# One-hot products for the last two expert groups, row gathers beside the experts, and four barriers fewer

## The chip, the cores and the metric

The kernel runs on one core of one Trainium2 chip. The metric is the device time of one launch in microseconds (us). All data are float32. TensorE is called PE in the profile, VectorE DVE, ScalarE ACT, GpSimd POOL, and the queue that loads weights SP.

## The reference, cut to what matters

512 tokens with 1024 features pass through one block of four small mixers with a dense feed-forward part, and then through two blocks of attention with a routed mixture of 16 experts. The change touches only the second half of each of the two routed layers (`l` is 0 or 1):

```python
x = layer_norm(ALPHA * x + mix, ln_g[l, 0], ln_b[l, 0])
ffn = routed_moe(x, router_w, router_b, moe_w_gate[l], moe_w_up[l], moe_w_down[l])
x = layer_norm(ALPHA * x + ffn, ln_g[l, 1], ln_b[l, 1])
```

`routed_moe` picks two experts for each token and weighs their outputs with two gates that sum to one: `y = y + gates[:, e:e+1] * (h @ w_down[e])` with `h = silu(xt @ w_gate[e]) * (xt @ w_up[e])`. The input of layer 1 is the layer norm that ends layer 0, with its gain `ln_g[0, 1]` and bias `ln_b[0, 1]`.

## The kernel before

Every engine runs the same list of stages (`STAGES`, L182): norm1, mixers, mix_out, up, down, gate, then for each of the two routed layers an attention half (even_in to even_out, odd_in to odd_out), route, experts, overflow and combine. Behind most stages the four compute engines meet: each drains, counts up one semaphore and waits for the others (`meet`, e.g. L536). `NO_MEET` (L190) lists the stages without such a barrier. SP stands outside the barriers and loads weights when a semaphore says that a buffer is free.

**Experts.** Each expert owns 96 rows (`CAP`), three tiles of 32. The 1536 rows are cut into 12 groups of 128 (`NG`), so one group holds rows of two experts. For each group POOL gathers the tokens' rows of x from DRAM (L2263), PE transposes them, multiplies with gate and up weights (`enter`, L955), transposes the hidden values (`turn_h`, L973) and multiplies with the down weights (`leave`, L963). The order on PE is enter(g), leave(g-1), turn_h(g), and at last leave(11). ACT copies the 128x1024 result of a group out of PSUM into one of two buffers `y_sb` and stores it to the DRAM tensor `expert_rows` (L1393 to L1402). The 96 MB of weights of a layer come through seven buffers of 2 MB, six of `ring` and `xT`, in an order worked out in advance (`PASSES`, `loads_of`); `FIRST_FREE` (L298) says in which order the buffers are first taken. `load_experts` (L2357) issues the loads on SP as the passes free buffers. Rows beyond 96 of an expert go to `overflow`, a loop over `over_n` slots that each engine reads into a register (`slots_of`, L318).

**Route.** DVE works out in some 80 small operations each token's two experts, ranks and places (`route`, L1935, and `place_tokens`, L2000, which runs at the start of the experts). Among them is `at_rank`, a 128x128 one-hot matrix per token tile and choice that PE multiplies with token numbers to get the list of tokens of each group (L924).

**Combine.** Behind the barriers of experts and overflow, POOL loads the layer norm's gain and bias rows (L2187), and then issues eight gathers of 128 rows from `expert_rows` (L2295; two choices, four token tiles). For each tile ACT weighs the first row (L1189), DVE adds the second with its weight (`mul_add`, L1517, called at L2063), adds `ALPHA * x` (L2064), and runs `norm_tile` (L1541): two batch statistics, aggregate, epsilon; ACT takes the root (L1147); DVE centres (L1557), inverts the root and applies gain and bias (L1569). In layer 0 PE transposes the finished tile (`turn_tile`, L556), and ACT copies it into xT (L1152), from which the next stage, `odd_in`, starts. In layer 1 SP writes each tile to the output.

**The attention stages' weights.** `chunks` are numbered weight pieces and chunk `at` lies in ring slot `at % RING`. The seven pieces of the odd attention (29 to 35) are loaded by `load` (L2327) once their slot's last holder among the experts is done. `odd_out` (`halves`, L755, on PE; `residual`, L1581, on DVE) multiplies with two halves of `w_o` and adds the residual.

Of the kernel before, what the change touches and what calls it, by code (L numbers as in the profile page):

```python
# [27 lines left out]
P = 128  # L28
T = 512
# [17 lines left out]
NG = E * CAP // P  # L47
OVER_K = -(-(T - CAP) // P)
# [37 lines left out]
def packs(i):  # L86
# [17 lines left out]
        ("token_f", (np.arange(NT)[None, :] * P + q[:, None]).astype(f)),  # L104
        ("norm1", cols(i["norm1_g"])),
# [84 lines left out]
NO_MEET = ("even_out", "route0", "odd_out", "route1")  # L190
# [6 lines left out]
def build(nc, w, pk_shapes, out, stop=None):  # L197
# [3 lines left out]
    with ctx:  # L201
# [28 lines left out]
        weight = sb("weight", [P, 2, NT])  # L230
# [58 lines left out]

        def experts_of(g):  # L290

            return [(4 * g + i) // 3 for i in range(4)]
# [5 lines left out]
        FIRST_FREE = [(5, 2, 0, 1, 3, 4, RING), (2, 3, 0, 1, 4, 5, RING)]  # L298
# [13 lines left out]

        def expert_buffer(b, k):
# [9 lines left out]
        def slot_view(at, c):  # L323
            nk, ncols = c[2], c[4]
            return ring[:, at % RING, 0:nk * ncols].rearrange("p (k n) -> p k n", k=nk)
# [33 lines left out]
        y_rows = Area().take(2, NT, D)  # L359
# [64 lines left out]
        scaled_p, probsT_done, sinks_in = sem("scaled_p"), sem("probsT_done"), sem("sinks_in")  # L424
        probsT_taken = sem("probsT_taken")
        pair_done, out_done, out_taken, bias_row = sem("pair_done"), sem("out_done"), sem("out_taken"), sem("bias_row")
# [8 lines left out]
        rows_gathered = [sem(f"rows_gathered{n}") for n in range(NT)]  # L435
        idx_cleared, idx_loaded, x_stored = sem("idx_cleared"), sem("idx_loaded"), sem("x_stored")
# [7 lines left out]
        first_weighed = sem("first_weighed")  # L444
# [49 lines left out]
        def summed(j):  # L494

            m = HC - j
            if j < 8:
# [25 lines left out]
        idx_one = sb("idx_one", [P, 1], U32)  # L523
        over_w = ea.take(2, SLOT)
        y_cleared = sem("y_cleared")

        over = {n: sem(f"over_{n}") for n in ("idx", "in", "xT_mm", "xT", "gate_up_mm", "silu", "h", "hT_mm", "hT", "down_in",
                                              "y_mm", "y", "stored", "passed", "all_stored")}
# [4 lines left out]
        def _(pe):  # L533
# [8 lines left out]
            def arrived(at):  # L542
                pe.wait_ge(w_loaded[at % RING], 16 * (at // RING + 1))
# [434 lines left out]

            def experts(l):

                turn_x(l, 0)
                for g in range(NG):
                    enter(l, g)
                    if g:
                        leave(l, g - 1)
                    turn_h(l, g)
                leave(l, NG - 1)

            def overflow(l):

                n, done = slots_of(pe, l)
                gate_w, up_w = (over_w[:, i, :].rearrange("p (k n) -> p k n", k=KD) for i in range(2))
                down_w = over_w[:, 0, :].rearrange("p (k n) -> p k n", k=4)
                with pe.If(n > 0):
                    with pe.Fori(0, n) as slot:
# [17 lines left out]
                        for i in range(2):  # L1013
                            product(banks[5 + i][:, :], [(hidT[:, t, :], down_w[:, t, i * 512:(i + 1) * 512])
                                                         for t in range(4)]).then_inc(over["y_mm"], 1)

            def combine(l):
                if l == 0:
# [99 lines left out]
        def _(act):  # L1118
# [37 lines left out]
            def norm_tiles(stage, before=None):  # L1156
                for n in range(NT + 2):
# [4 lines left out]
                    if n >= 2 and stage not in FEATURE_GAIN and stage != "combine1":  # L1162
# [23 lines left out]
            def combine(l):  # L1186
                def weigh_first(n):
                    act.wait_ge(rows_gathered[n], 32 * (l + 1))
                    A(y_rows[:, 0, n, :], y_rows[:, 0, n, :], ACT.Copy, scale=weight[:, 0, n:n + 1]).then_inc(first_weighed, 1)  # L1189

                norm_tiles(f"combine{l}", weigh_first)
# [187 lines left out]
            def experts(l):  # L1379
                take_x(NG * l)  # L1380
                for g in range(NG):
# [5 lines left out]
                    if g:  # L1387
                        leave(l, g - 1)
                leave(l, NG - 1)
                for b in range(2):  # L1390
                    act.wait_ge(y_stored[b], 16 * (NG // 2) * (l + 1))

            def leave(l, g):  # L1393

                at = NG * l + g
                if at >= 2:
                    act.wait_ge(y_stored[g % 2], 16 * (at // 2))
# [3 lines left out]
                act.wait_ge(y_taken, 2 * at + 2)  # L1401
                act.dma_start(y_dram[g * P:(g + 1) * P, :], y_sb[:, g % 2, :]).then_inc(y_stored[g % 2], 16)  # L1402

            def overflow(l):
                n, done = slots_of(act, l)
                with act.If(n > 0):
                    with act.Fori(0, n) as slot:
# [7 lines left out]
                        for g in range(2):  # L1415
                            act.wait_ge(over["y_mm"], j * 2 + g + 1)
                            step_in(A(y_sb[:, 0, g * 512:(g + 1) * 512], banks[5 + g][:, :], ACT.Copy), j * 2 + g + 1)
                        act.dma_start(y_dram[bass.ds(slot * P + NG * P, P), :], y_sb[:, 0, :]).then_inc(over["stored"], 16)

                    act.wait_ge(over["stored"], (n + done) * 16 + 16)  # L1420
                    act.sem_inc(over["all_stored"], 1)
# [77 lines left out]
        def _(dve):  # L1499
# [81 lines left out]
            def residual(name, scale, loads=0):  # L1581

                f = F[name]
                for k in range(10):
                    if k < 8:
# [349 lines left out]
            def route(l):  # L1935
# [62 lines left out]
                V.tensor_copy(idx_sb[:, 0:NG], banks[5][:, 0:NG]).then_inc(idx_ready, 1)  # L1998

            def place_tokens(l):  # L2000
# [25 lines left out]
                step(V.reciprocal(wsum, wsum))  # L2026
                for j in range(2):
                    step(V.tensor_tensor(weight[:, j, :], weight[:, j, :], wsum, ALU.mult))
# [8 lines left out]
                step(V.tensor_copy(over_list[:, :], e_list))  # L2037

            def experts(l):
                place_tokens(l)  # L2040
                for at in range(NG * l, NG * (l + 1)):
# [4 lines left out]
                    V.tensor_copy(hidT.rearrange("p a b -> p (a b)"), banks[4][:, :]).then_inc(hT_ready, 1)  # L2046

            def overflow(l):
                n, done = slots_of(dve, l)
                with dve.If(n > 0):  # L2050
                    with dve.Fori(0, n) as slot:
# [5 lines left out]
                        V.tensor_copy(hidT.rearrange("p a b -> p (a b)"), banks[4][:, :]).then_inc(over["hT"], 1)  # L2057

            def combine(l):
                for n in range(NT):  # L2060
# [373 lines left out]
```

## Time and profile before

| | us |
|---|---|
| median of 3 runs | 2189.02 (2188.75 to 2190.48) |
| the profiled execution | 2186.29 |
| its span, first to last instruction | 2184.6 |
| PE / DVE / ACT / POOL busy | 1953.7 / 658.8 / 398.3 / 81.1 |

The times are device times of whole launches. The span is that of one execution that was recorded instruction by instruction; its own time is 1.7 us above its span. PE is busy for 89% of the span; the granted TensorE clock was 0.928 of full speed on average. The DMA queues moved 336.59 MB.

### The profile page before, as it was taken

What the parts mean: (1) busy time and instruction counts of PE and PEld (TensorE: products, weight loads), DVE (VectorE), ACT (ScalarE), POOL (GpSimd) and SP (SyncE); (2) the same over time, 40 slices, a digit from 0 to 9 for tenths busy, and PEclk for the clock granted to TensorE, in tenths of its full rate; (3) what the DMA queues carried; (4) which work ended last, traced back from release to release, by engine and by line L of the source; (5) the groups of instructions that cost most, each with busy time, mean ns of one, the idle gap of its engine ahead of it and who ended that gap; (6) DMA issues with size and microseconds to landing.
All of it is one profiled execution on the core that took longest, in us unless ns stands there. A gap on an engine that the chain in (4) does not pass through costs nothing.

```text
span 2184.6 us, 23031 instructions
## 1 busy us (share of the span) xinstructions
PE 1953.7 (89%) x9622; PEld 877.2 (40%) x9622; DVE 658.8 (30%) x1564; ACT 398.3 (18%) x853; POOL 81.1 (4%) x104
## 2 busy tenths in 40 slices
PE   7999999999999998979997999955988997999991
PEld 3454444444444444435552333312644444333230
DVE  3736312233200331116343000005676625000005
ACT  3213011111100022016410111101125511111111
POOL 0000010000000000000002000010000000200001
PEclk9989999999999999987897999986999996999996
DMA  4104532221212213110234999963100233899973
GB/s 147 64 20 145 183 135 77 77 77 68 77 58 77 71 39 116 39 39 1 97 131 155 392 398 399 394 246 128 39 0 1 78 145 135 279 398 398 395 293 154
DMA packets 140920, 336.59 MB, mean 154 GB/s; under 512 B 4568, under 2 KB 12776, under 8 KB 140688
## 3 DMA queue, kind: packets, MB, share of 16 engines
q1 hardware_dynamic: 126384, 283.80, 35.3%
q0 software_dynamic: 10688, 36.71, 4.4%
q10 hardware_dynamic: 3744, 14.59, 1.6%
q8 instruction: 78, 1.28, 0.2%
q14 instruction: 26, 0.21, 0.0%
HBM read 310.93 MB, written 24.14 MB: 153 GB/s over the span
## 4 chain that ended last, share of the span: by engine, by line
PE 76%; issue 8%; DMA 7%; DVE 6%; ACT 2%; POOL 0%; DVEq 0%; another core or an unknown queue 0%; POOLq 0%; PEldq 0%; ACTq 0%; SPq 0%
PE psum L553 31%; PE psum L951 20%; PE psum L796 7%; DMA ring<-in_moe_w_up 5%; PE psum L733 5%; PE psum L862 3%; PE psum L890 2%; PE psum L875 2%; PE psum L932 1%; DVE small L1546 1%; PE psum L565 1%; DMA scratch<-expert_rows,place 1%; PE psum L675 1%; ACT ring L1357 1%; DVE x L1517 1%
## 5 line engine op out<-in xcount | busy, mean ns | idle before, releaser
L951 PE MATMUL psum<-ring,scratch 128*32 128x512 f32 x3840 | 518.1, 602 | 13.3 <-DMA ring<-in_moe_w_up 8.9
L553 PE MATMUL psum<-xT,ring 128*128 128x512 f32 (+2 forms) x1056 | 465.5, 601 | 8.2 <-PE psum L553 3.4
L553 PEld LDWEIGHTS psum<-xT,ring 128*128 128x128 f32 (+2 forms) x1056 | 199.5, 190 | 271.7 <-issue 270.8
L951 PEld LDWEIGHTS psum<-ring,scratch 128*32 128x32 f32 x3840 | 144.3, 111 | 301.5 <-issue 296.4
L553 PE MATMUL psum<-ring,xT 128*128 128x512 f32 (+4 forms) x704 | 239.8, 497 | 2.5 <-ACTq L1124 1.6
L553 PEld LDWEIGHTS psum<-ring,xT 128*128 128x128 f32 x704 | 120.3, 194 | 120.0 <-issue 111.8
L796 PE MATMUL psum<-ring,scratch 128*128 128x512 f32 x352 | 155.7, 603 | 4.0 <-remote 3.3
L951 PE MATMUL psum<-xT,scratch 128*32 128x512 f32 x768 | 129.3, 603 | 8.4 <-DMA ring<-in_moe_w_up 8.4
L1517 DVE SCALAR_TENSOR_TENSOR scratch<-psum,overlay,scratch 128x511 f32<-128x511 f32 x88 | 65.9, 749 | 232.0 <-ACT scratch L1288 230.4
L2044 DVE TENSOR_TENSOR scratch<-psum,scratch 128x512 f32<-128x512 f32 x24 | 16.6, 692 | 345.9 <-PE psum L951 345.9
L733 PE MATMUL psum<-xT,ring 128*128 128x512 f32 x224 | 104.4, 623 | 2.4 <-DVEq L1506 2.3
L796 PEld LDWEIGHTS psum<-ring,scratch 128*128 128x128 f32 x352 | 67.4, 193 | 91.6 <-issue 91.6
L1517 DVE SCALAR_TENSOR_TENSOR x<-x,psum 128x512 f32<-128x512 f32 x32 | 22.0, 688 | 269.0 <-PE psum L796 141.2
L862 PE MATMUL psum<-scratch 64*128 64x256 f32 (+11 forms) x256 | 76.4, 522 | 14.9 <-POOLq L2171 10.2
L1288 ACT ACTIVATE scratch<-psum,overlay 128x512 f32<-128x512 f32 x44 | 34.2, 777 | 270.2 <-PE psum L553 270.2
L553 PE MATMUL psum<-ring,scratch 128*128 128x512 f32 x160 | 72.6, 606 | 2.9 <-DVEq L1506 1.6
L1147 ACT ACTIVATE small<-small 128x1 f32<-128x1 f32 x28 | 5.7, 203 | 377.2 <-DVE small L1553 377.2
L1345 ACT ACTIVATE ring<-ring,small 128x257 f32<-128x257 f32 (+5 forms) x128 | 68.0, 538 | 8.1 <-DVE small L1905 8.0
L2046 DVE COPY scratch<-psum 128x512 f32<-128x512 f32 x24 | 16.6, 692 | 172.9 <-PE psum L976 172.9
L565 PE MATMUL psum<-base,x 128*128 128x128 f32 x128 | 22.3, 334 | 51.4 <-DVE x L1569 46.9
L733 PEld LDWEIGHTS psum<-xT,ring 128*128 128x128 f32 x224 | 44.5, 201 | 57.2 <-issue 56.9
L1377 ACT ACTIVATE scratch<-psum 128x512 f32<-128x512 f32 x48 | 26.3, 595 | 210.9 <-PE psum L932 210.9
(339 smaller groups left out, 1612.8 us busy)
## 6 DMA issues: line engine op xcount, KB each, us to landing
ring<-in_moe_w_gate SPq DMA_DIRECT2D x28, 2048.0 KB, 15.1
ring<-in_moe_w_up SPq DMA_DIRECT2D x28, 2048.0 KB, 17.4
ring<-in_moe_w_down SPq DMA_DIRECT2D x24, 2048.0 KB, 15.6
ring<-in_w_up SPq DMA_DIRECT2D x11, 2048.0 KB, 7.7
xT<-in_moe_w_down SPq DMA_DIRECT2D x8, 2048.0 KB, 11.5
expert_rows<-scratch ACTq DMA_DIRECT2D x24, 512.0 KB, 7.4
ring<-in_w_down SPq DMA_DIRECT2D x4, 2048.0 KB, 7.8
ring<-in_even_w_in SPq DMA_DIRECT2D x4, 2048.0 KB, 7.6
```

The costliest lines, as they stand in the source:

```text
L553: mm = nc.tensor.matmul(out_, lhsT, rhs, start=(j == 0), stop=(j == len(pairs) - 1))
L565: mm = nc.tensor.transpose(banks[turn_bank(stage, n) + j][:, t * P:(t + 1) * P], src[:, (4 * j + t) * P:(4 * j + t + 1) * P], ident)
L733: mm = nc.tensor.matmul(banks[k % 2][:, :], lhsT, rhs, start=(t == 0), stop=(t == KD - 1))
L796: mm = nc.tensor.matmul(banks[4 * half_ + n][:, :], hidden[:, k0 + t, n * P:(n + 1) * P], w_[:, t, :], start=(k0 + t == 0), stop=(k0 + t = ...
L862: mm = nc.tensor.matmul(banks[2 * (p % 2) + hh][:, 0:span(kind, n)[1]], head_q(kind, n, j, hh), head_k(kind, n, j, hh), start=True, stop=True)
L875: mm = nc.tensor.transpose(banks[4 + u % 2][:, b * P:(b + 1) * P], probs[:, u % 6, b * P:(b + 1) * P], ident)
L890: mm = nc.tensor.matmul(banks[6 + g % 2][r, c], head_v(kind, s0 // P + b, h), probsT[:, (2 * p + hh) % 4, b * P:(b + 1) * P], start=(b == ...
L951: mm = nc.tensor.matmul(bank[r, :], lhsT[:, t, r], w_[:, t, c0:c0 + 512], start=(t == 0), stop=(t == nk - 1))
L1288: A(conv[:, k % 4, :], banks[k % 8][:, :], ACT.Identity, bias=operand["fconv_b"][:, k:k + 1], scale=w3[:, k, 2:3]).then_inc(f.a, 1)
L1345: A(to, of, ACT.Exp, bias=negmax[:, u % 8:u % 8 + 1], accum_out=p_total[:, u % 8:u % 8 + 1])\
L1377: A(xgT[:, 4 * h:4 * h + 4, :].rearrange("p a b -> p (a b)"), banks[h][:, :], ACT.Copy).then_inc(xgT_ready, 1)
L1517: return V.scalar_tensor_tensor(out_, in0, s, in1, ALU.mult, ALU.add)
```

## The change

- `NE = NG - 2 = 10`. Groups 0 to 9 are stored to DRAM as before. Groups 10 and 11 are not stored; they stay in the two buffers `y_sb`, and their slots in `expert_rows` are zeroed at the start, together with those of the overflow (12 clearing DMAs of 512 KB in the stage `up`, before 10).
- The eight row gathers are issued at the end of POOL's `experts`, once the stores of groups 0 to 9 have landed, into a memory area of their own (the overflow's weight buffers). DVE adds them to x behind its last work on the experts, eight `mul_add` of 128x1024, with weights that are zero for places outside the ten groups.
- `share_late` on PE, between enter(0) and turn_h(0): eight one-hot products of 2 columns that give each row of groups 10 and 11 its gate weight. `seek_late` on DVE, behind its first group: two matrices `late_hot` of 128x512, row by token, that hold the weight where row and token belong together.
- `combine`: PE multiplies `late_hot` with `y_sb` into PSUM, for each of four token tiles two groups and two halves (16 products of 128x512). DVE adds PSUM to x and sums the row in one operation; ACT squares the centred row and sums it, and takes the root. In layer 0 DVE only centres and scales x; gain and bias are applied feature by feature where the transposed tile is copied into xT, half of it by ACT, half by DVE. The gain and bias that x itself still lacks are applied in `odd_out`, on the first four steps of `residual` (`gain`). In layer 1 gain and bias rows are loaded into a ring slot after the last gate pass.
- The weights are divided by ALPHA in `place_tokens`, so that `ALPHA * x` is no step of its own; the epsilon is divided by ALPHA squared.
- experts0, overflow0, experts1 and overflow1 join `NO_MEET`; each engine reads the overflow count near the end of `experts`.
- The odd attention's pieces lie in slots 2, 3, 1, 4, 5, 2, 3, and `FIRST_FREE` of layer 1 is 4, 5, 0, 1, 2, 3 with xT last.

```diff
+NE = NG - 2
-NO_MEET = ("even_out", "route0", "odd_out", "route1")
+NO_MEET = ("even_out", "route0", "experts0", "overflow0", "odd_out", "route1", "experts1", "overflow1")
...
+        ODD_SLOTS = (2, 3, 1, 4, 5, 2, 3)
-        FIRST_FREE = [(5, 2, 0, 1, 3, 4, RING), (2, 3, 0, 1, 4, 5, RING)]
+        FIRST_FREE = [(5, 2, 0, 1, 3, 4, RING), (4, 5, 0, 1, 2, 3, RING)]
...
+            def share_late(l):
+                pe.wait_ge(late_w, l + 1)
+                for j in range(2):
+                    for n in range(NT):
+                        mm = nc.tensor.matmul(banks[7][:, 0:2], at_rank[:, j, n, :], late_share[:, NT * j + n, :],
+                                              start=(j == 0 and n == 0), stop=(j == 1 and n == NT - 1))
+                mm.then_inc(late_mm, 1)
...
                     enter(l, g)
-                    if g:
+                    if g == 0:
+                        share_late(l)
+                    else:
                         leave(l, g - 1)
                     turn_h(l, g)
+                pe.wait_ge(over_known, l + 1)
+                slots[l] = slots_of(pe, l)
                 leave(l, NG - 1)
...
             def combine(l):
+                for n in range(NT):
+                    for g in range(2):
+                        for h in range(2):
+                            if n == 0 and h == 0:
+                                pe.wait_ge(late_ready, 2 * l + g + 1)
+                            if n == 0:
+                                pe.wait_ge(y_taken, 2 * (NG * l + NE + g) + h + 1)
+                            mm = nc.tensor.matmul(banks[2 * n + h][:, :], late_hot[g][:, n * P:(n + 1) * P],
+                                                  y_sb[:, g, h * 512:(h + 1) * 512], start=(g == 0), stop=(g == 1))
+                    mm.then_inc(late_done, 1)
                 if l == 0:
                     for n in range(NT):
                         turn_tile("combine0", n)
...
+                def spread(n):
+                    act.wait_ge(tile_var, base + n + 1)
+                    step(A(y_rows[:, 0, n, :], x[:, n, :], ACT.Square, bias=mean[:, n:n + 1], accum_out=sumsq[:, n:n + 1]))
+                    A(rstd[:, n:n + 1], sumsq[:, n:n + 1], ACT.Sqrt, scale=1.0 / D, bias=moe_eps).then_inc(tile_sd, 1)
+                def take(n):
+                    act.wait_ge(tile_turned, base + n + 1)
+                    for k in range(KD // 2):
+                        ins = A(xT[:, k, n * P:(n + 1) * P], banks[2 * n][:, k * P:(k + 1) * P], ACT.Identity,
+                                scale=operand["moe_g"][:, k:k + 1], bias=operand["moe_b"][:, k:k + 1])
+                    ins.then_inc(tile_taken, 1)
...
+                slots[l] = slots_of(dve, l)
+                for n in range(NT):
+                    dve.wait_ge(rows_gathered[n], 32 * (l + 1))
+                    step(mul_add(x[:, n, :], y_rows[:, 0, n, :], early_weight[:, 0, n:n + 1], x[:, n, :]))
+                    mul_add(x[:, n, :], y_rows[:, 1, n, :], early_weight[:, 1, n:n + 1], x[:, n, :]).then_inc(early_added, 1)
...
+                def gather_sum(n):
+                    dve.wait_ge(late_done, NT * l + n + 1)
+                    step(V.tensor_tensor_reduce(x[:, n, :], psum[:, 2 * n:2 * n + 2, :].rearrange("p b q -> p (b q)"), x[:, n, :],
+                                                1.0, 0.0, ALU.add, ALU.add, total(n)))
+                    V.tensor_scalar(back(n), total(n), -1.0 / D, None, ALU.mult).then_inc(tile_var, 1)
+                    if l == 1:
...
+                        centred[n] = begun(V.scalar_tensor_tensor(y_rows[:, 1, n, :], x[:, n, :], back(n), end_g, ALU.add, ALU.mult))
+                def scale(n):
+                    r = rstd[:, n:n + 1]
+                    dve.wait_ge(tile_sd, base + n + 1)
+                    step(V.reciprocal(r, r))
+                    if l == 0:
+                        V.tensor_scalar(x[:, n, :], x[:, n, :], back(n), r, ALU.add, ALU.mult).then_inc(tile_ready, 1)
+                    else:
+                        finished(centred[n])
+                        V.scalar_tensor_tensor(x[:, n, :], y_rows[:, 1, n, :], r, end_b, ALU.mult, ALU.add).then_inc(tile_ready, 1)
+                def take(n):
+                    dve.wait_ge(tile_turned, base + n + 1)
+                    for k in range(KD // 2, KD):
+                        V.tensor_scalar(xT[:, k, n * P:(n + 1) * P], banks[2 * n + 1][:, (k - 4) * P:(k - 3) * P],
+                                        operand["moe_g"][:, k:k + 1], operand["moe_b"][:, k:k + 1], ALU.mult, ALU.add)
+                for n in range(NT + 2):
+                    if n < NT:
+                        gather_sum(n)
+                    if 1 <= n <= NT:
+                        scale(n - 1)
+                    if n >= 2 and l == 0:
+                        take(n - 2)
...
+                def gain(n):
+                    dve.wait_ge(moe_rows, 32)
+                    step(V.tensor_tensor(x[:, n, :], x[:, n, :], affine_g, ALU.mult))
+                    step(V.tensor_tensor(x[:, n, :], x[:, n, :], affine_b, ALU.add))
...
+                pool.wait_ge(late_ready, 2 * (l + 1))
+                if l == 1:
+                    pool.wait_ge(gate_up_done, 2 * (NG * l + NG - 1) + 1)
+                    for i, n in enumerate(("ln_g_1_1", "ln_b_1_1")):
+                        pool.dma_start(ring[:, END_ROWS, i * D:(i + 1) * D], w[n]).then_inc(moe_rows, 16)
+                for b in range(2):
+                    pool.wait_ge(y_stored[b], 16 * (NE // 2) * (l + 1))
+                gather_rows(lambda n: rows_gathered[n])
```

## Rows read from the trace of the kernel before

**Rows 1.** The chain that ended last, layer 0: start us, us, what.
```profile
1423.29 20.74 PE psum L951 x192
1445.40 7.12 PE psum L951 x64
1453.17 7.24 DMA expert_rows<-scratch
1465.62 10.55 DMA scratch<-expert_rows,place
1508.67 31.83 PE psum L553 x112
```

**Rows 2.** The same chain, layer 1.
```profile
2108.94 20.74 PE psum L951 x192
2138.81 2.62 DMA expert_rows<-scratch
2147.47 4.96 DMA scratch<-expert_rows,place
2153.72 1.30 DVE scratch L1517
2174.52 1.29 DVE scratch L1517
2180.24 1.29 DVE x L1569
```

**Rows 3.** Stretches of 10 us: engine busy (x instructions), granted clock, DMA share, GB/s.
```profile
1190.00:1200.00 10.00, 9.76 (x80) 2.87 (x76) 0.00 (x0) 0.60 (x1) 5.78 (x6) 1.00 0.37 54
1200.00:1210.00 10.00, 10.00 (x91) 3.42 (x82) 0.69 (x1) 1.83 (x4) 1.06 (x2) 1.00 1.04 364
...
1430.00:1440.00 10.00, 10.00 (x99) 3.00 (x94) 0.69 (x1) 0.60 (x1) 0.00 (x0) 1.00 0.26 106
...
1460.00:1470.00 10.00, 0.00 (x0) 0.00 (x0) 0.00 (x0) 0.00 (x0) 5.60 (x7) 0.50 1.05 406
...
1510.00:1520.00 10.00, 10.00 (x20) 3.21 (x19) 1.37 (x2) 0.00 (x0) 0.00 (x0) 0.84 0.01 2
```

**Rows 4.** POOL in order of time, layer 1, the last of eight gathers.
```profile
2154.95 0.94 POOL L2295 DMA_INDIRECT scratch<-expert_rows,place  x1 [0.30 <-issue]
```

**Rows 5.** DMA issues: median us to landing; gathers of layer 0, then layer 1.
```profile
expert_rows<-scratch ACTq DMA_DIRECT2D x24, 512.0 KB, 7.4
...
scratch<-expert_rows,place POOLq DMA_INDIRECT x8, 12.6
...
scratch<-expert_rows,place POOLq DMA_INDIRECT x8, 5.8
```

**Rows 6.** Groups of instructions by form: x count | busy us, mean ns.
```profile
L1517 DVE SCALAR_TENSOR_TENSOR scratch<-scratch,weight 128x1024 f32<-128x1024 f32 x8 | 10.2, 1280 | 54.8 <-ACT scratch L1189 54.8
L1901 DVE CUSTOM_DVE_ANT_0 ring<-psum,base 128x512 f32<-128x512 f32 x16 | 10.4, 689 | 8.2 <-PE psum L862 8.2
L1564 DVE TENSOR_SCALAR scratch<-x,small 128x1024 f32<-128x1024 f32 x8 | 6.0, 753 | 0.3
L1176 ACT ACTIVATE scratch<-x 128x1024 f32<-128x1024 f32 x4 | 4.2, 1056 | 4.1 <-DMA x<-in_x 3.9
L1357 ACT ACTIVATE ring<-psum 128x128 f32<-128x128 f32 x32 | 7.3, 275 | 11.9 <-PE psum L875 11.8
L1147 ACT ACT_TABLE_LOAD x10 | 12.8, 1283 | 3.0 <-DVEq L1506 2.4 <-ACTq L1124 0.3
```

**Rows 7.** PE in order of time: products at L924, transposes at full clock.
```profile
1133.82 1.07 PE L565 MATMUL psum<-base,x 128*128 128x128 f32 x8
...
1156.50 3.58 PE L924 MATMUL psum<-scratch 128*128 128x12 f32 x16 [2.93 <-DVE scratch L1995]
```

**Rows 8.** The chain: a count read into PE's register, and odd_out's first half.
```profile
1460.64 0.49 PEldq L320
...
1757.55 27.74 PE psum L553 x64
```

More of the change, by code:

```diff
@@ L104, in packs @@
         ("token_f", (np.arange(NT)[None, :] * P + q[:, None]).astype(f)),
+        ("tile_row", rows(np.arange(NT, dtype=f) * P)),
+        ("moe_g", cols(i["ln_g_2"][0, 1])), ("moe_b", cols(i["ln_b_2"][0, 1])),
         ("norm1", cols(i["norm1_g"])),
@@ L311, in build @@
                     holder[b] = LAST_USE[m, e], PASSES[LAST_USE[m, e]]
+        END_ROWS = buffer_of[1]["gate", E - 1][0]
+        assert END_ROWS < RING and LAST_USE["gate", E - 1] == PASSES.index(("gate", NG - 1))
         def expert_buffer(b, k):
@@ L1161, in norm_tiles @@
                         root_tile(stage, n)
-                    if n >= 2 and stage not in FEATURE_GAIN and stage != "combine1":
+                    if n >= 2 and stage not in FEATURE_GAIN:
                         take_tile(stage, n - 2)
@@ L1416, in overflow @@
                             act.wait_ge(over["y_mm"], j * 2 + g + 1)
[L1417 to L1421, printed above, removed]
+                            step_in(A(y_over[:, g * 512:(g + 1) * 512], banks[5 + g][:, :], ACT.Copy), j * 2 + g + 1)
+                        act.dma_start(y_dram[bass.ds(slot * P + NG * P, P), :], y_over).then_inc(over["stored"], 16)
             def step_in(ins, value):
@@ L1579, in take_tile, with residual @@
                 ins.then_inc(tile_taken, 1)
-            def residual(name, scale, loads=0):
+            def residual(name, scale, loads=0, first=None):
                 f = F[name]
                 for k in range(10):
+                    if first and k < NT:
+                        first(k)
                     if k < 8:
@@ L2141, in out_stage @@
             def out_stage(name, loads):
-                residual(name, ALPHA, loads)
+                def gain(n):
+                    dve.wait_ge(moe_rows, 32)
+                    step(V.tensor_tensor(x[:, n, :], x[:, n, :], affine_g, ALU.mult))
+                    step(V.tensor_tensor(x[:, n, :], x[:, n, :], affine_b, ALU.add))
+                residual(name, ALPHA, loads, gain if name == "odd_out" else None)
             run = {
@@ L2289, in overflow @@
                         pool.dma_start(over_w[:, 0, :].rearrange("p (k n) -> p k n", k=4), src[0]).then_inc(over["down_in"], 16)
[L2291 to L2297 removed]
+                    pool.wait_ge(over["stored"], (n + done) * 16 + 16)
+                    pool.sem_inc(over["passed"], 1)
+                    gather_rows(lambda n: over_rows[l])
             run = {
```

155 lines of the change are left out of this document (105 added, 50 removed).

## The prediction

> **What bounds the kernel now.** I read the chain of waits first, at the end of either routed layer, then the table of 10 us stretches, then POOL's and the DMA issues' rows, and last the prices by form. The chain shows one serial tail per layer. In layer 0, PE's last product of the experts starts at 1445.40 and ends at 1452.5; ACT copies; the store takes 7.24; the engines meet; the first gathers take 10.55 more; then DVE works through four tiles; odd_in's first product starts only at 1508.67 [rows 1]. So 56 us pass between the end of the experts and the next stage, in which PE does nothing but transposes: its busy time is 0.00 and its clock 0.50 at 1460 to 1470 [rows 3]. Layer 1 has the same tail, from 2138.2 to 2184.6, with faster transfers (2.62 and 4.96) and one tile each 6.93 us (from 2153.72 to 2174.52 it is three tiles) [rows 2]. Before the tail the experts are bound by the DMA engines: from about 1200 the DMA share is 1.04, and only at 1430 to 1440 does it fall to 0.26 [rows 3]. The change works on both tails, and puts a little into the stretch that feeds the DMA-bound phase.
>
> All that follows is in the clock of the profiled execution.
>
> **Layer 0, what is added ahead of the tail.** `share_late` is eight products with a full 128x128 left side and 2 columns. The nearest row is L924, the same left side with 12 columns, 16 records (eight products) in 3.58, at a low clock [rows 7]; eight transposes at full clock, 1.07, are the low end. PE is at full clock there [rows 3], so I take about half of 3.58, 1.9. It stands on PE before turn_h(0), where DVE has the hidden values ready at about the same time, so nothing covers it. Whether it is paid depends on the DMA engines: at 1190 to 1200 their share is only 0.37 [rows 3], because the loads wait for buffers that PE frees. The loads start 1.9 later and the DMA-bound phase moves along: +1.9, with zero and 3.6 as ends. `place_tokens` grows by four small operations behind work that already ends before the first group's hidden values are needed; they and `seek_late` (two comparisons and two scalings of 128x512, some 2.5 us on DVE once per layer) are hidden in PE's 13.9 us of the next gate and up products. The register reads (0.49 is the longest one in the chain [rows 8]) come while PE waits for DVE's copy of the last hidden values; what sticks out I take as 0.1 in layer 0 and 0.5 in layer 1, where two counts are read, and the branch around the overflow as 0.3 each.
>
> **Layer 0, the tail anew.** PE: down(11) ends at 1452.5 + 1.9 + 0.4 = 1454.8. The 16 late products cost as much each as odd_out's, 27.74 for 64 records or 32 products [rows 8], 0.867: 3.5 per token tile, 13.9 in all. They follow without a gap, so at full clock. Tile 0 is there at 1458.3, tile 3 at 1468.7.
> DVE: free when down(11) starts, 1447.3, plus 0.9 for its register read. Eight additions of 128x1024 at 1.280 [rows 6] with 0.03 between them are 10.5: 1458.7, just with tile 0.
> The gathers: down(9) ends where the 20.74 of 192 records begin, 1423.3 [rows 1]; with 1.9, ACT's copy and a store of 7.4 [rows 5] that is 1433.2. Eight issues at 0.94 + 0.30 [rows 4] last until 1443.1. They move 4.2 MB. The odd pieces come beside them: two (3.55 MB) once gate(11) is done at 1432.1, two more (2.9 MB) seven us later. Together 10.6 MB at 406 GB/s [rows 3] take 26 us; with half the engines the gathers need 4.2 / 0.203 = 20.7 and are in at about 1454. Counted by landings it is 1443.1 + 12.6 [rows 5] = 1455.7. DVE wants the last tile at 1448.2 + 7.9 = 1456.1. It fits, barely; a few us of delay would still be covered by PE's late products, until 1468.7.
> The end: PE transposes only behind all late products, so from 1468.7. Four transposed tiles cost 1.07 each at full clock [rows 7]. From there DVE sets the pace: take(0) begins at 1469.9 and costs 1.1 (four pieces of 128x128; only ACT has a row for such a piece, 0.275 [rows 6]; I take it for DVE too, between 0.8 and 1.5 for the four). gather_sum is twice the 0.689 of the summing operation from PSUM, less one overhead, and a small one: 1.45. scale is 0.753 for a 128x1024 TENSOR_SCALAR and a reciprocal: 0.95 [rows 6]. ACT's square (1.056 and 0.19 for the sum) and one table load of 1.283 [rows 6] lie behind PE's first tiles. So 1469.9 + take 1.1 + sum(3) 1.45 + scale(2) 0.95 + take 1.1 + scale(3) 0.95 + take 1.1 + take 1.1 = 1477.7, 0.5 for a last transpose that is late, 0.7 for the meeting: odd_in starts at 1478.9 instead of 1508.67. **Layer 0 gives 29.8.**
>
> **Between the layers.** `gain` puts eight DVE operations of 128x1024, about 1.23 each or 9.8, on the first four steps of odd_out, where PE needs 27.74 for the first half [rows 8] and DVE has 0.7 of work per tile. Its row loads wait behind nothing but two others on POOL; even landing 15 us late they leave DVE level with PE by the fourth tile. Cost 0; uncovered it would be 9.8. The ring order: piece 34 now waits for 29 and 35 for 30, both used up more than 100 us before odd_out; layer 1's first expert buffers are again those of the two latent pieces. Cost 0. Two more clearing DMAs lie in `up`, 0.
>
> **Layer 1.** share_late again 1.9, reads and branch 0.8. down(11) starts at 2108.94 + 20.74 + 1.37 (the same gap as in layer 0) = 2131.05 and ends at 2138.2 [rows 2]. PE has tile 0 at 2138.2 + 2.7 + 3.5 = 2144.4 and tile 3 at 2154.8. POOL waits for gate(11), 2115.9 + 1.9, loads two rows (1.2), issues gathers from 2119.3 to 2129.2; landing 5.8 [rows 5], 2135. DVE: 2131.0 + 1.9 + 1.3 = 2134.2, additions to 2144.7, branch to 2145.0. Then per tile sum 1.45, centring 1.25, reciprocal 0.1, scaling 1.25: 4.05, of which PE's 3.5 and ACT's 1.5 are covered; four are 16.2: 2161.2. Behind DVE's last operation come 3.1 for the output (2180.24 + 1.29 to 2184.6 [rows 2]): 2164.3. **Layer 1 gives 20.3.**
>
> **Sum.** 29.8 + 20.3 = 50.1; the profiled execution's 2186.3 becomes 2136.2. The median of the runs lies 2.7 above it, so I forecast 2139.
>
> **Two rules of the Trainium skill.** POOL's gather issues keep their 0.94 us and a pitch of 1.24 up to the last one at 2154.95 [rows 4], although DVE's additions had run since 2153.72 [rows 2]. The Trainium skill, SBUF — State Buffer, section "SBUF: two separate sides", speaks against this change: while VectorE runs an operation in a two-port mode, GpSimd can't write the descriptors of its DMAs, which then start late. By that rule gathers beside DVE work would stretch; by the row they don't beside SCALAR_TENSOR_TENSOR, and in the new place DVE has 0.69 us of PSUM work in 7 us. The sum would be the same unless other modes come in.
> The first pair of gathers took 10.55 beside the odd pieces and 4.96 alone [rows 1, 2]. The Trainium skill, DMA: Bandwidth & Descriptors, section "Queues, rings and completion order", says that a DMA engine takes turns between the queues that have work, a packet at a time. By it the gathers get half; packets of unequal size would make it less, which is the first rival.
>
> **Rivals.**
> *Gathers late in layer 0* (15%). For it: 12.6 against 5.8 [rows 5]. Against: PE's late products cover until 1468.7. If the gathers get through only behind the odd pieces' 6.4 MB (16 us), the last lands at 1470; DVE ends its additions at 1472.6 and has four tiles of 3.5 and a transpose before it, 1488.4: 9.5 less gain, 2148.5.
> *Late products at half clock* (7%). The clock was 0.50 in this place before [rows 3], but behind 10 idle us. If the waits at tile 0 let it fall, 32 products cost 27.8 more, all on the path: 2167.
> *The change doesn't do what it says* (4%): the gathers still start only behind the experts. Then only the barriers (about 4 each) and DVE's shorter tiles remain: layer 0 8.7, layer 1 4.6, 2176.
> *Slower* (3%): the clock doesn't come back. Late products at half clock take 27.8 of the 50.1, and if PE stays there into odd_in, each us of its full-clock work costs one more. It decides from 22 us of such work on; a chain stretch like the 31.83 at 1508.67 [rows 1] and the next one would make 2139 + 27.8 + 60 = 2227. Against it: before, the clock was back at 0.84 over 1510 to 1520 [rows 3], after longer idleness.
>
> **How the numbers follow.** The forecast holds 70%; 1% is for small debts that cancel it. The low end is its own with share_late and reads at nothing (-5), odd_in finding the clock up (-2) and takes at 0.8 (-2), and a little more: 2128. The high end takes in late gathers and most of a half-clock tail: 2162; 5% lie above for the serial case and the slower one, 4% partly above for half clock, a few below. A change within 0.2% (4.4 us) can't be told from none by this measurement: 1%. Faster 96%, slower 3%.
>
> **What would show it.** In the trace after: eight gathers on POOL that begin near 1433 and near 2119; a block of late products of 13.9 us right behind down(11) at clock 1.00, with no store between; odd_in's first product some 24 us behind the end of down(11), not 56; each layer 1 tile about 4.05 us apart on DVE instead of 6.93; the DMA-bound phase as long as before and some 2 us later. Wrong: PE idle ahead of the late products, DVE waiting for gathers beyond 1459, an expert phase that grew by more than 3 us, or a PE wait in odd_out for DVE.

## Result and the profile after

The changed kernel runs in 2131.7 us (median of 4, 2130.6 to 2134.1) against 2189.8 (median of 4): a ratio of 0.9741, 95% interval 0.9728 to 0.9754. It is faster by 58 us. The forecast was 50 us faster, 2139, with a range of 2128 to 2162. The profiled execution has a span of 2129.4, 55.2 below that of before.

The chain of waits of the changed kernel, both tails (start us, us, what; the lines that answer to [rows 1] and [rows 2]):

```profile
1155.12 4.20 DMA scratch<-x_rows,idx_sb
...
1417.96 20.74 PE psum L978 x192
1440.07 7.07 PE psum L978 x64
1447.15 13.93 PE psum L1072 x32
1471.63 34.98 PE psum L580 x112
1506.61 10.24 PE psum L1095 x24
...
1724.96 27.74 PE psum L580 x64
...
2076.46 20.74 PE psum L978 x192
2098.56 7.07 PE psum L978 x64
2105.64 7.08 PE psum L1072 x16
```

The store, the gathers and the barriers have left the chain. In layer 0 the late products (L1072) stand right behind down(11), and odd_in starts 24.5 us behind that product's end, where it was 56. In layer 1 the chain leaves PE after two tiles and goes on over DVE. Its timeline (start us, us, engine, line, operation), with POOL's first gathers of either layer:

```profile
1426.40 0.93 POOL L2442 DMA_INDIRECT scratch<-expert_rows,place  x1 [63.56 <-DMA expert_rows<-scratch]
...
2085.53 0.99 POOL L2442 DMA_INDIRECT scratch<-expert_rows,place  x1 [0.30 <-issue]
```

```profile
1440.26 7.64 DVE L1591 SCALAR_TENSOR_TENSOR x<-scratch,early_weight,x 128x1024 f32<-128x1024 f32 x6 [0.24 <-issue]
1448.06 2.61 DVE L1591 SCALAR_TENSOR_TENSOR x<-scratch,early_weight,x 128x1024 f32<-128x1024 f32 x2 [0.16 <-DMA scratch<-expert_rows,place]
1450.82 1.23 DVE L2181 CUSTOM_DVE_ANT_0 x<-psum,x 128x1024 f32<-128x1024 f32 x1 [0.15 <-PE psum L1072]
...
2099.11 10.15 DVE L1591 SCALAR_TENSOR_TENSOR x<-scratch,early_weight,x 128x1024 f32<-128x1024 f32 x8 [0.60 <-issue]
...
2116.79 1.22 DVE L2181 CUSTOM_DVE_ANT_0 x<-psum,x 128x1024 f32<-128x1024 f32 x1
...
2120.83 1.22 DVE L2181 CUSTOM_DVE_ANT_0 x<-psum,x 128x1024 f32<-128x1024 f32 x1
```

All eight row sets are there in time: in layer 0 DVE waits 0.16 us for one of them, in layer 1 for none, and its eight additions end just as PE has the first tile. In layer 1 a tile takes 4.04 us on DVE (2116.79 to 2120.83) instead of 6.93 [rows 2]. PE's clock behind the experts, in stretches of 10 us (busy, granted clock, DMA share, GB/s; compare [rows 3]):

```profile
1440.00:1450.00 10.00, 9.93 (x71) 3.42 (x72) 9.46 (x9) 1.19 (x2) 0.00 (x0) 1.00 1.04 401
1450.00:1460.00 10.00, 10.00 (x24) 4.37 (x23) 6.57 (x14) 5.22 (x8) 0.00 (x0) 1.00 0.58 222
1460.00:1470.00 10.00, 5.89 (x35) 4.43 (x33) 7.13 (x21) 6.64 (x19) 0.00 (x0) 0.85 0.00 0
1470.00:1480.00 10.00, 8.37 (x14) 2.51 (x15) 1.23 (x4) 1.37 (x4) 1.04 (x2) 0.64 0.01 2
```

Where the span's 55.2 us went, stage by stage, from the two chains:

| stretch | before | after | less by |
|---|---|---|---|
| start to the first token gather of layer 0 | 1160.57 | 1155.12 | 5.4 |
| experts 0, to the start of group 11 | 262.72 | 262.84 | -0.1 |
| group 11 to odd_in's first product | 85.38 | 53.67 | 31.7 |
| odd_in to odd_out's first product | 248.88 | 253.33 | -4.4 |
| odd_out and route 1 | 86.19 | 86.28 | -0.1 |
| experts 1, to the start of group 11 | 265.20 | 265.22 | 0.0 |
| group 11 to the end | 75.66 | 52.94 | 22.7 |

The two tails give 54.4. The first row and the fourth are stretches in which the change adds next to no work (two clearing DMAs in the first block); the experiments tell the two apart. Single times of one kernel spread by up to 18 us in the later measurements (2183.5 to 2201.3 for the kernel of before), so the traces' stretches carry the verdicts below and the medians stand beside them. "Tail 0" and "tail 1" are the table's third and last stretch.

### The profile page after: what moved, and what is told of

It reads as the page before. It is cut to its first block, busy times and chain, and to the rows that moved or that the text cites. A ratio compares the mean times of both kernels' runs of the same rounds, so it can differ in the third digit from the quotient of the medians.

```text
span 2129.4 us, 23221 instructions
## 1 busy us (share of the span) xinstructions
PE 1977.8 (93%) x9718; PEld 890.7 (42%) x9718; DVE 671.2 (32%) x1600; ACT 402.5 (19%) x869; POOL 82.1 (4%) x106
## 4 chain that ended last, share of the span: by engine, by line
PE 79%; issue 8%; DMA 6%; DVE 5%; ACT 2%; POOL 0%; DVEq 0%; another core or an unknown queue 0%; ACTq 0%; POOLq 0%; SPq 0%
PE psum L580 32%; PE psum L978 20%; PE psum L823 7%; DMA ring<-in_moe_w_up 5%; PE psum L760 5%; PE psum L889 3%; PE psum L917 2%; PE psum L902 2%; PE psum L1072 1%; PE psum L959 1%; PE psum L702 1%; PE psum L592 1%; ACT ring L1429 1%; PE psum L1003 0%; PE psum L1095 0%
## 5 line engine op out<-in xcount | busy, mean ns | idle before, releaser
L978 PE MATMUL psum<-ring,scratch 128*32 128x512 f32 x3840 | 513.9, 602 | 14.4 <-DMA ring<-in_moe_w_up 11.4
L823 PEld LDWEIGHTS psum<-ring,scratch 128*128 128x128 f32 x352 | 67.4, 193 | 91.6 <-issue 91.6
L889 PE MATMUL psum<-scratch 64*128 64x256 f32 (+11 forms) x256 | 77.1, 529 | 14.2 <-POOLq L2326 10.2
L917 PE MATMUL psum<-ring,scratch 128*64 128x128 f32 x592 | 52.3, 308 | 9.3 <-ACT ring L1429 9.1
```

Of the source, the lines that this page charges most:

```text
L823: mm = nc.tensor.matmul(banks[4 * half_ + n][:, :], hidden[:, k0 + t, n * P:(n + 1) * P], w_[:, t, :], start=(k0 + t == 0), stop=(k0 + t = ...
L889: mm = nc.tensor.matmul(banks[2 * (p % 2) + hh][:, 0:span(kind, n)[1]], head_q(kind, n, j, hh), head_k(kind, n, j, hh), start=True, stop=True)
L917: mm = nc.tensor.matmul(banks[6 + g % 2][r, c], head_v(kind, s0 // P + b, h), probsT[:, (2 * p + hh) % 4, b * P:(b + 1) * P], start=(b == ...
L978: mm = nc.tensor.matmul(bank[r, :], lhsT[:, t, r], w_[:, t, c0:c0 + 512], start=(t == 0), stop=(t == nk - 1))
```

## Experiments

**Both kernels again.** No edit.

> The changed kernel once more, to see what of the difference belongs to the change. The profile of the change shows the first block (up to the even attention's product at 1069.21) 5.4 us earlier than before, at a granted clock that fell less often in the mixers; no edit touches that part. If that is chance of the clock's phase, first-block ends will spread by several us from one execution to the next, of either kernel. If it belongs to the program (another length of the code or another layout), every kernel with this first block ends it near 1069, and the one of before near 1074.6. Time by both: 2131 to 2134 us.

> The kernel of before once more with a profile. If the first block's 5.4 us belong to the program, the even attention's product begins near 1074.6 again and odd_in's first product needs about 31.8 us for its 112 records again; if they are chance of the clock's phase, one or the other differs by some us.

Measured: 2135.3 us for the change (4 runs, 2127.5 to 2137.3) against 2186.5 (7 runs), ratio 0.9754 (0.9721 to 0.9788), a gain of 51.1 where the first measurement had 58.0; and one profiled run of before, 2188.6. The chains, first of the change, then of before:

```profile
1160.07 4.17 DMA scratch<-x_rows,idx_sb
...
1476.90 34.96 PE psum L580 x112
```

```profile
1157.70 4.20 DMA scratch<-x_rows,idx_sb
...
1509.08 31.85 PE psum L553 x112
```

The first gather starts at 1160.1 now where it was 1155.1, in the same kernel, and at 1157.7 in the kernel of before where it was 1160.6. Over the eleven traces of kernels with the changed first block (two of the change and nine of its variants) it lies near one of three values, 1154.5 to 1155.1, 1157.5 to 1157.9 or 1160.1 to 1161.2, and both traces of before fit the same values. So the 5.4 us are chance. PE's busy time up to 1150 goes with it, from 1076.8 to 1081.9 us, so PE's work takes longer in the late ones. The 3.1 us more in odd_in's first 112 records are not chance: 31.83 and 31.85 before, 34.96 to 34.99 in all eight traces with the change and no filler; the filler experiment shows where they lie. The tails repeat within 0.1 (53.66 and 52.91) for the change and within 0.8 for before.

**The barriers back.**

```diff
-NO_MEET = ("even_out", "route0", "experts0", "overflow0", "odd_out", "route1", "experts1", "overflow1")
+NO_MEET = ("even_out", "route0", "odd_out", "route1")
```

> The changed kernel with the four barriers behind experts and overflow put back (two per layer). Theory (the barriers' removal is worth something because it lets PE's late products start beside DVE's additions of the gathered rows): PE can start them only when DVE is through with its additions, 3 to 4 us after down(11), plus two meetings of 0.5 to 1 us: 4 to 6 us per layer, 8 to 12 in all, 2141 to 2144 us. Rival (barriers cost only their own semaphores, some 1 us each): 2 to 4 us, 2134 to 2136.

Measured: 2147.2 us (11.8 above the change measured beside it); tail 0 60.5 (+6.8), tail 1 59.9 (+7.0). The chain, and PE's clock in stretches of 4 us:

```profile
1448.71 1.28 DVE x L1591
...
1450.88 16.63 PE psum L1072 x32
```

```profile
1448.00:1452.00 4.00, 1.12 (x2) 0.63 (x3) 1.96 (x2) 0.00 (x0) 0.00 (x0) 0.68 1.05 390
1452.00:1456.00 4.00, 4.00 (x6) 1.55 (x5) 0.00 (x0) 0.00 (x0) 0.00 (x0) 0.50 0.67 263
```

The theory's direction holds, and its size was too small: 4 to 6 us per layer were expected. PE waits for the end of DVE's additions, 4.2 us in all, and then its late products take 16.63 instead of 13.93, at a clock that had fallen to 0.50 behind that wait; this 2.7 was no term of the theory. From the end of the additions (1449.99) to the first late product are 0.9 us: the barriers' own semaphores are the smallest part.

**The gathers behind the experts.**

```diff
+                pool.wait_ge(y_taken, 2 * NG * (l + 1))
                 gather_rows(lambda n: rows_gathered[n])
```

> The changed kernel, but POOL issues the row gathers only when ACT has taken the last expert group out of PSUM, so nothing of them lies beside the experts. Theory (the overlap of the gathers is the largest part of the gain): layer 0 ends its additions near 1466 instead of 1450.7 and loses about 11 us after what PE's late products cover, layer 1 about 14 us: 2131.7 + 25 = 2157, between 2150 and 2162. Rival (PE's late products of 13.9 us cover them anyway): below 2140.

Measured: 2155.4 us (20.1 above the change measured beside it); tail 0 65.4 (+11.7), tail 1 67.7 (+14.7), 26.4 together. DVE now waits for the transfers:

```profile
1463.14 2.61 DVE L1591 SCALAR_TENSOR_TENSOR x<-scratch,early_weight,x 128x1024 f32<-128x1024 f32 x2 [14.99 <-DMA scratch<-expert_rows,place]
1466.72 7.71 DVE L1591 SCALAR_TENSOR_TENSOR x<-scratch,early_weight,x 128x1024 f32<-128x1024 f32 x6 [0.97 <-DMA scratch<-expert_rows,place]
```

Both tails moved as expected. The traced execution, 2164.5, is the slowest of the four, though; the others lie at 2152.8 to 2157.0. So the overlap of the gathers is worth 26 us by the trace, about half of the 54.4, and 20 by the medians; one trace can't say which is typical.

**Late products twice.**

```diff
                 for n in range(NT):
+                    for _ in range(2):
                     for g in range(2):
```

(with the loop's body indented)

> The changed kernel with every group of late one-hot products done twice (the second overwrites the first, same output). Theory for layer 0: PE's late products are on the path as a whole (transposes stand behind them), so all 13.9 us more show. For layer 1: DVE's 4.05 us per tile is the pace now and PE's 3.5 hides under it; doubled, PE's 6.9 becomes the pace, and the end moves by about 12.5. Sum 26, 2158 us. Rival (DVE's additions and its four tiles are the path in both layers, PE is beside them): less than 14 us in all.

Measured: 2159.8 us (24.5 above the change); tail 0 67.4 (+13.7), tail 1 65.5 (+12.5). Both numbers are those of the theory:

```profile
1452.71 27.66 PE psum L1073 x64
...
2121.83 27.68 PE psum L1073 x64
2149.53 1.22 DVE x L2182
```

In layer 0 every us of late products is paid. In layer 1 the last sum now starts as PE's last product ends (2149.53), and 1.2 of the 13.7 added are hidden; that they lay under DVE's 4.04 per tile is the theory's reading of it.

These three experiments don't cover the whole tail. What the store that left the chain (7.24 and 2.62 us [rows 1, 2]) and the shorter work per tile gave by themselves, and what the new places of the weights in the ring did, no run tells apart.

**The 2-column products more often.** `share_late` repeats its eight products 4 and 12 times.

```diff
+                for _ in range(4):
                 for j in range(2):
```

> The changed kernel with the one-hot products of 2 columns behind the first group done four times (same result), 5.5 us more on PE per layer, ahead of turn_h(0). The forecast took the single ones as paid in full (1.9 per layer), because the loads there wait for buffers that PE frees; the trace shows an expert phase no longer than before. Theory (the weight stream sets the phase's length and PE has some 10 us of waits for it per layer, so delays near its start are absorbed): below 3 us in all. Rival (the delay moves the loads along, and a single 1.84 happened to fall in a gap): about 11 us.

> The same products twelve times, 20 us more on PE per layer. By the theory that the weight stream hides PE's delay up to about 10 us per layer, some 10 us per layer show, 20 in all (12 to 28). By the rival that the delay moves the loads along, all of it shows, 40 us. If even this costs nothing, PE is nowhere near the bound in the experts.

Measured: 2157.9 and 2208.5 us. With x4 the expert phases are 272.9 and 271.2 (+9.3 and +7.6 on the mean of 263.6 over the seven traces with single products at the first group, 262.1 to 265.2; PE's products became 7.7 and 7.5 longer). Another 5 us lie in the odd attention of that execution (258.2), where the granted clock was 0.90 over its last 42 us and 1.00 in the change; this is not explained. With x12 the phases are 300.5 and 299.4, 36 to 37 more, where the products became 34.9 longer. The theory of the first text (below 3 us) is wrong and its rival is right: what PE loses here is paid in full. And PE loses more than the count says, so that the rival's 11 and 40 us were too small as well. In order of time, x12:

```profile
1184.58 36.77 PE L1013 MATMUL psum<-scratch 128*128 128x2 f32 x192
```

and its stretches:

```profile
1190.00:1200.00 10.00, 10.00 (x48) 10.00 (x48) 0.00 (x0) 0.00 (x0) 5.65 (x6) 0.50 0.18 53
1200.00:1210.00 10.00, 10.00 (x49) 10.00 (x48) 0.00 (x0) 0.00 (x0) 0.25 (x1) 0.50 0.20 53
1210.00:1220.00 10.00, 10.00 (x49) 10.00 (x48) 0.00 (x0) 0.00 (x0) 0.00 (x0) 0.50 0.01 2
```

A record costs 0.191 us, against 0.149 in x4 and 0.115 in the single set: PE is busy all the time, with weight loads of 128x128 and two columns behind each, and the granted clock is 0.50. The DMA share falls to 0.01: SP issues no weight load from 1190 to 1225, since its loads wait for buffers that PE frees.

**The 2-column products at the ninth group.**

```diff
-                    if g == 0:
-                        share_late(l)
-                    else:
+                    if g:
                         leave(l, g - 1)
+                    if g == 8:
+                        share_late(l)
...
-                    if at == NG * l:
+                    if at == NG * l + 8:
                         seek_late(l)
```

> The changed kernel with the one-hot products of 2 columns (and what DVE makes of them) moved from the first group to the ninth, where PE has waits for the weight stream behind it. Done 4 and 12 times at the first group they cost as much as PE's own time, and yet the change's expert phases (262.8 and 265.2 us from the first gather to the last group) are no longer than those of before (262.7 and 265.2; 265.7 and 265.4 in another execution). Theory (the single 1.84 us is paid, and hidden in the 3 us by which the phase varies): the phases become about 1.8 shorter each, near 261.5 on average, 3.7 us of the time. Rival (a delay below some us is absorbed because the stream isn't waiting for just these buffers): no difference.

Measured: 2132.2 us (6 runs, 2131.4 to 2138.9), phases 261.5 and 264.3; with the last kernel's 261.8 and 264.4 (below) a mean of 263.0 against 263.6. The theory's 1.8 per phase did not show, but this is inconclusive: 0.6 us lies well inside the spread of 3, and 1.8 can't be excluded.

**Filler products.**

```diff
                 if l == 0:
+                    def fill(count):
+                        pe.wait_ge(tile_taken, norm_base["combine0"] + 1)
+                        for _ in range(count):
+                            nc.tensor.matmul(banks[0][:, :], ident, causal, start=True, stop=True)
                     for n in range(NT):
                         turn_tile("combine0", n)
+                        if n:
+                            fill((0, 2, 1, 2)[n])
```

> The changed kernel with five products of 128x512 on PE that nobody reads, put into the gaps between the transposes in layer 0's combine (two after tile 1, one after tile 2, two after tile 3), so that PE is not idle ahead of odd_in. In the change's trace odd_in's first 112 records need 34.98 us against 27.7 + 3 at full clock, and the clock is 0.50 at 1472 to 1476 and again near 1500. Theory (the clock fell because of the gaps, the low stretch at the start can be bought off): 2 to 4 us faster than the change, clock near 1.00 at odd_in's start. Rival (the low stretches come with the kind of work, or wherever the clock's phase falls): no faster; or slower by up to 1 us where a filler delays a transpose.

> The filler kernel once more beside the other two: its median was level with the change's although its trace showed 6.4 us less behind the filler. Theory: the gain is real and was covered by the first block's chance 6 us; 2126 to 2130 us here, and 246.9 again from odd_in's to odd_out's start. Rival: the filler only sometimes keeps the clock up; then this trace shows about 253.

Measured: 2132.2 us (5 runs, 2123.8 to 2136.2; ratio to before 0.9740, 0.9724 to 0.9757) and 2129.6 (4 runs; 0.9732, 0.9698 to 0.9767). The stretches of the first:

```profile
1464.00:1468.00 4.00, 3.63 (x16) 1.74 (x15) 3.89 (x13) 3.38 (x9) 0.00 (x0) 1.00 0.02 4
1468.00:1472.00 4.00, 3.69 (x15) 1.70 (x14) 2.22 (x7) 2.36 (x7) 0.97 (x2) 1.00 0.00 0
1472.00:1476.00 4.00, 4.00 (x10) 1.23 (x9) 0.00 (x0) 0.00 (x0) 0.07 (x1) 1.00 0.00 0
...
1496.00:1500.00 4.00, 4.00 (x26) 4.00 (x25) 0.00 (x0) 0.17 (x1) 0.00 (x0) 0.65 0.02 4
```

The clock stays at 1.00 until some 24 us into odd_in; its first 112 records take 29.43 and 31.19 instead of 34.97, and the stretch from odd_in to odd_out is 246.9 and 248.2, against 253.0 to 253.3. So the filler gives 5 to 6 us in the traces, where 2 to 4 were expected. In the medians it lies between 0.5 above and 5.8 below the change, which these runs don't separate.

The 112 records are 48 of 512 columns and then 64 of four columns. Split there (us from first start to first start, and to the end), the loss of the change and the gain of the filler lie in different places:

| | the 48 | the 64 |
|---|---|---|
| before, two traces | 23.10, 23.31 | 8.73, 8.54 |
| change without filler, eight traces | 23.37 to 23.68 | 11.31 to 11.59 |
| with filler, two traces | 20.82, 20.82 | 8.61, 10.37 |

The 64, in order of time, before and after, and the clock over a part of them:

```profile
1531.77 8.73 PE L553 MATMUL psum<-ring,xT 128*128 128x4 f32 x64
1495.20 11.40 PE L580 MATMUL psum<-ring,xT 128*128 128x4 f32 x64
```

```profile
1531.80:1536.00 4.20, 4.20 (x40) 4.20 (x38) 0.89 (x2) 0.35 (x2) 0.00 (x0) 1.00 0.00 0
1536.00:1540.40 4.40, 4.40 (x28) 4.40 (x27) 0.00 (x0) 0.17 (x1) 0.00 (x0) 0.63 0.00 0
```

```profile
1495.00:1499.00 4.00, 4.00 (x30) 3.79 (x29) 0.89 (x2) 0.17 (x1) 0.00 (x0) 0.83 0.00 0
1499.00:1503.00 4.00, 4.00 (x20) 4.00 (x21) 0.00 (x0) 0.17 (x1) 0.00 (x0) 0.50 0.00 0
```

The low clock at odd_in's start, worth 2.3 to 2.9 us, was there before the change too; the filler buys it off. What the change loses against before lies in the 64: the clock falls to 0.50 under them in both kernels, but earlier in the change. With the filler it falls late again in the first trace and somewhere between in the second. Why it comes earlier in the change no run shows.

**All three together**, with another order in layer 0's combine:

```diff
+                    for job, n in ((gather_sum, 0), (gather_sum, 1), (scale, 0), (gather_sum, 2), (scale, 1), (gather_sum, 3), (scale, 2),
+                                   (take, 0), (scale, 3), (take, 1), (take, 2), (take, 3)):
+                        job(n)
...
+                for n in range(NT):
+                    spread(n)
+                for n in range(NT if l == 0 else 0):
+                    take(n)
```

> The changed kernel with three edits: the one-hot products at the ninth group, the filler products in layer 0's combine, and another order there on DVE and ACT (sum of tile 3 ahead of the first copies into xT; ACT's squares ahead of its copies). The filler gave 6.4 us between odd_in's start and odd_out's start in its trace (246.9 against 253.3). The new order should bring odd_in's start from 53.0 to 51 us behind the last group's start. Theory by sum: 6.4 + 2 + up to 3.7 = 8 to 12 us under the change, 2121 to 2125 us in the median. Rival (the granted clock's phase takes back what the filler gives): within 3 us of the change.

Measured: 2134.5 us (6 runs; ratio 0.9745, 0.9718 to 0.9772), no better than the change, where 2121 to 2125 were expected. The trace says more than the median: counted from the first token gather to the end, this execution has 967.0 us against 974.3 and 973.4 for the change, but its first block was among the late ones (1161.2). The 7 us are the filler's gain (247.1 from odd_in to odd_out); with the filler alone the same count is 967.6 and 967.7. The new order gave nothing: tail 0 is 54.2, with 53.0 in the filler's traces and 51 expected. The trace shows why: PE's filler (L1079) waits for ACT's first copy, which the new order puts behind all squares, and tile 2's transpose is queued behind the filler.

```profile
1468.90 0.29 ACT small L1256
1469.19 1.41 ACT xT L1261 x4
```

```profile
1470.64 1.98 PE L1079 MATMUL psum<-base 128*128 128x512 f32 x4 [2.76 <-ACT xT L1261]
1472.46 1.04 PE L592 MATMUL psum<-base,x 128*128 128x128 f32 x8
```

The two edits were not compatible; the order without the filler wasn't run.

## Why the prediction was right

**The tails were sized step by step, and held.** From group 11's start to odd_in's the forecast has 1478.9 - (1423.3 + 1.9) = 53.7; the trace has 53.67. For layer 1 it is 53.5 and 52.94. The terms: late products 13.9 and 13.93; additions 10.5 and 10.4; sum from PSUM 1.45 and 1.41; scaling 0.95 and 0.92; first gather 1433.2 and 1431.8 (1426.4, with the 5.4 of the first block added back); landing 12.6 and 10.6; a layer 1 tile 4.05 and 4.04. A take, the copy of a transposed tile into xT, was 1.1 for DVE and is 1.37 for four pieces, ACT 1.50; the path behind the late products is 10.55 against the forecast's 10.2, so that layer 0's 53.67 hits 53.7 because this 0.35 makes up for the 0.4 of the register read below. `gain` in odd_out cost nothing, as forecast (86.28 against 86.19).

**Too dear.** The register reads and branches, 0.4 and 0.8, cost nothing: from group 11's start to down(11)'s it is 22.11 in layer 0 and 22.10 in layer 1 with the reads, and 22.11 without them. On DVE the additions begin 0.19 and 0.55 behind down(11)'s start, where 0.9 and 1.3 were forecast. `share_late` is 1.84 long (forecast 1.9), but the forecast's 3.8 for both layers don't show in the phases (-0.1 and 0.0). That such a delay is paid there is shown for 7.7 us and more; for the single one it stays open, hidden in a spread of 3 us.

**Too cheap.** odd_in's start was costed at nothing, and at -2 in the low end: I expected the clock no worse than before. It costs about 4 us in every trace of the change without filler (253.0 to 253.3 against 248.9 and 249.5; 258.2 in the x4 kernel). By the rows it is the granted clock, but not at odd_in's start, where the clock came back as before: of these 4 us 2.8 lie in the 64 products of four columns, 0.3 in the 48 ahead of them, and the rest behind.

**What is luck in the total.** The tails gave 0.5 more than forecast, share_late's 3.8 did not show, and odd_in took 4.4: these nearly cancel, and so the gain behind the first token gather is 49.8 in the profiled pair, with 50.1 forecast. The second pair gives 55.7 by the same count (53.3 as a whole). The medians gave 58.0 and then 51.1, and the median that was to lie 2.7 above the profiled execution lay 0.7 above it. So the true gain is known only to several us, and that 50.1 lies near one of the pairs is partly chance.

**The rivals.** Late gathers: no, 0.16 us of waiting; wholly behind the experts they cost 11.7 and 14.7 in one trace, where the forecast's milder form had 9.5 in layer 0 alone. Late products at half clock: no, 13.93 at 1.00; with a wait of some 4 us ahead of them, in the barrier kernel, 2.7 us of this rival came true. The change doesn't do what it says: no, gathers at 1426 and 2085. Slower, because the clock doesn't come back: no, odd_in's first 48 records took 23.57 against 23.10; the clock's 4.4 came later and were small beside this rival's 88. The Trainium skill's rule that VectorE in a two-port mode keeps GpSimd from writing descriptors (SBUF — State Buffer, "SBUF: two separate sides") was hardly put to the test in the new place: DVE ran one operation of 0.69 us beside the eight issues, which took 0.93 to 0.94 us in layer 0 and 0.94 to 0.99 in layer 1. With the gathers behind the experts, where they stood beside DVE's additions, the last two issues took 1.00 and 1.01 in layer 0, 1.10 and 1.02 in layer 1. The Trainium skill's rule that DMA engines take turns between queues (DMA: Bandwidth & Descriptors, "Queues, rings and completion order") is not contradicted: the gathers landed in 10.6 us in layer 0, where the other queues moved 7.7 MB from 1420 to 1450, and in 6.6 in layer 1, where they moved 2.1 MB from 2080 to 2110. No run tests the turns themselves.

## What to carry to other kernels

A serial tail behind a phase (store, barrier, gather, add) is worth reading link by link: here its links could go beside work already there, and the gain of the tails could be summed from rows of the same trace. Keep what is made last on the chip and bring it to its place with products, and let only the older part take the way through DRAM; then the last product, not the last store, opens the next stage. Where a tail gets shorter, look at the clock all through the stage behind it and not only at its start, and compare stretches between fixed points of two traces rather than whole spans, when the rest of the kernel varies by chance.

## What the runs showed of the hardware

PE ran 192 records of two columns, with PE and its weight loads busy all 10 of 10 us, and the granted clock was 0.50 over 1190 to 1220; a record took 0.191 us there, 0.149 among 64 and 0.115 among 16. Under 64 products of four columns, again with PE busy throughout, the clock fell to 0.50 in both kernels, and they took 8.6 or 11.4 us by how early it fell. Five products that nobody reads, in gaps of 1 to 3 us, kept the clock at 1.00 and shortened the next 48 records from some 23.5 us to 20.82 in both traces. A wait of 4.2 us ahead of 32 wide records made them 16.63 us instead of 13.93. The first block of the kernel, to which the variants add nothing, ends anywhere in a range of 6.7 us from one execution to the next, near one of three values.
